# Product-key experts in one interleaved pass, and in two stages with half of the v rows read densely

## What is computed

```python
q = (hblk @ w_q).reshape(b_, PEER_BLOCK, PEER_HEADS, 2, PEER_QDIM // 2)
s1 = einsum('bthd,hnd->bthn', q[..., 0, :], k1)
s2 = einsum('bthd,hnd->bthn', q[..., 1, :], k2)
v1, i1 = lax.top_k(s1, PEER_TOPK)
v2, i2 = lax.top_k(s2, PEER_TOPK)
cand = v1[..., :, None] + v2[..., None, :]
cidx = i1[..., :, None] * PEER_NKEYS + i2[..., None, :]
score, pos = lax.top_k(cand, PEER_TOPK)      # over the 256 sums
idx = take_along_axis(cidx, pos)
gate = jax.nn.softmax(score, axis=-1)
act = jax.nn.gelu(einsum('bthkd,btd->bthk', w_u[idx], hblk))
out = einsum('bthk,bthkd->btd', gate * act, w_v[idx])
```

## Time and profile before

| | |
|---|---|
| median of 3 runs | 2938.45 us (2937.06 to 2939.99) |
| span of the profiled execution | 2939.0 us |
| first dot, last u gather | 1631.9 us, 2869.7 us |
| read from memory in the span | 898 MB |
| busy: PE, DVE, ACT, POOL | 2628.4, 1949.4, 979.2, 556.7 us |

### The profile page before, as it was taken

The page is one execution under the profiler, slowest core; times in us unless marked ns, Lnnn a source line. Parts: engine busy times, 40 slices in busy tenths (PEclk is TensorE's granted clock), DMA queues, the critical chain, the costliest instruction groups (busy, mean ns, idle before and its releaser), DMA issues.

```text
span 2939.0 us, 30782 instructions
## 1 busy us (share of the span) xinstructions
PE 2628.4 (89%) x11045; PEld 1777.7 (60%) x11045; DVE 1949.4 (66%) x2654; ACT 979.2 (33%) x1335; POOL 556.7 (19%) x580
## 2 busy tenths in 40 slices
PE   7999998999999999999999897777878877777777
PEld 3588886888777899998888753332434333232232
DVE  4679997444676788887555866666556656556646
ACT  5577776433564443334444211111101111111110
POOL 0000000000000000000000453433333333333333
PEclk9999999999999999999999999999999999999999
DMA  8733334542425888887566899999999999999998
GB/s 351 278 108 114 114 129 158 189 170 101 154 90 233 332 322 335 322 336 279 203 247 266 357 422 421 421 421 421 421 421 421 421 421 421 421 421 422 422 421 342
DMA packets 126356, 901.77 MB, mean 307 GB/s; under 512 B 14000, under 2 KB 15536, under 8 KB 17200
## 3 DMA queue, kind: packets, MB, share of 16 engines
q0 software_dynamic: 82944, 604.02, 49.8%
q1 hardware_dynamic: 38448, 276.84, 25.1%
q10 hardware_dynamic: 4864, 19.61, 1.7%
HBM read 898.29 MB, written 2.13 MB: 306 GB/s over the span
## 4 chain that ended last, share of the span: by engine, by line
PE 53%; DMA 35%; DVE 6%; issue 4%; ACT 1%; POOL 0%; POOLq 0%; SPq 0%; ACTq 0%; DVEq 0%
DMA u<-in_peer_u,idx 32%; PE ps L476 12%; PE ps L519 8%; PE ps L521 8%; PE ps L520 8%; PE ps L491 6%; DVE u L2042 3%; PE ps L882 2%; DMA v<-in_peer_v,idx 2%; PE ps L599 2%; PE ps L905 1%; DMA w<-in_stream 1%; PE ps L533 1%; PE ps L711 1%; PE ps L694 1%
## 5 line engine op out<-in xcount | busy, mean ns | idle before, releaser
L905 PE MATMUL ps<-v,dg 128*128 128x512 f32 x1920 | 894.4, 614 | 252.3 <-DMA v<-in_peer_v,idx 212.2
L2042 DVE SCALAR_TENSOR_TENSOR u<-u,hN 128x2048 f32<-128x2048 f32 x256 | 586.6, 2292 | 459.8 <-DMA u<-in_peer_u,idx 459.4
L905 PEld LDWEIGHTS ps<-v,dg 128*128 128x128 f32 x1920 | 356.4, 194 | 784.9 <-issue 427.9
L1383 DVE TENSOR_TENSOR wl<-w,wh 128x1024 fp32r<-128x1024 f32 x428 | 519.7, 1222 | 359.2 <-ACT wh L1018 358.8
L1018 ACT ACTIVATE wh<-w 128x1024 fp32r<-128x1024 f32 x428 | 451.3, 1059 | 607.9 <-PE ps L521 405.6
L2148 POOL DMA_INDIRECT u<-in_peer_u,idx x256 | 257.6, 1006 | 933.0 <-DVE u L2042 543.5
L476 PE MATMUL ps<-both,wh 128*128 128x256 f32 x2048 | 371.8, 284 | 0.0
L1326 ACT ACTIVATE dg<-con,wt 128x128 f32<-128x128 f32 x240 | 92.7, 399 | 807.4 <-PE ps L905 802.4
L476 PEld LDWEIGHTS ps<-both,wh 128*128 128x128 f32 x2048 | 320.1, 192 | 3.5 <-issue 3.3
L476 PE MATMUL ps<-both,wl 128*128 128x256 f32 x1024 | 289.8, 283 | 0.0
L2132 POOL DMA_DIRECT2D mr<-in_wmod x64 | 34.1, 534 | 1322.8 <-DVE br_lo L1791 912.7
(11 more groups left out here) (297 smaller groups left out, 2893.5 us busy)
## 6 DMA issues: line engine op xcount, KB each, us to landing
w<-in_stream SPq DMA_DIRECT2D x258, 1024.0 KB, 4.9
mr<-in_wmod POOLq DMA_DIRECT2D x64, 1024.0 KB, 6.9
wg<-in_gates ACTq DMA_DIRECT2D x8, 512.0 KB, 3.2
wx<-in_stream SPq DMA_DIRECT2D x4, 1024.0 KB, 7.9
u<-in_peer_u,idx POOLq DMA_INDIRECT x256
v<-in_peer_v,idx POOLq DMA_INDIRECT x256, 18.0
xs<-in_ctx ACTq DMA_DIRECT2D x1, 2048.0 KB, 7.6
xs<-in_x ACTq DMA_DIRECT2D x1, 2048.0 KB, 14.6
```

Source lines behind the costliest of these rows:

```text
L905: last = mm(ps[:, b, :], dg[:, k % 4, :], V[n % NV][:, b * 512:(b + 1) * 512], start=(k == 0), stop=(k == TOPK - 1))
L1383: tt(wl[p % SPLITS][:, :, :], W[s][:, q * PIECE:(q + 1) * PIECE, :], wh[p % SPLITS][:, :, :].bitcast(F32), ALU.subtract)\
L2042: stt(U[n % NU][:, :], U[n % NU][:, :], 1.0, hN[t][:, :], ALU.mult, ALU.mult, accum_out=dot[:, t, k:k + 1])\
```

## The change

The expert part is cut into two stages. In the first, only u rows are gathered, in the order of `ORDER`: both halves of head 0, then heads 1 to 7 of half 0, then those of half 1. There are eight u buffers. Of each group from the third on, the ranks 3, 8 and 13 (`ON_POOL`, without the last) are not dots of VectorE: GpSimd multiplies the tile with `hN[t]` in place (`product`), and ScalarE sums over the columns (`row_sum`). The others stay on VectorE with `U` and `hN`, both in SBUF. Results are kept in `dot` [128, 2, 128] for all heads, and weights are made once for each half.

The v table is split by columns. Its first DC = 1024 columns are read densely: 128 blocks of 128 rows x 1024 columns, in an order made on the host. For this the weights of all chosen experts are turned into a matrix for each token: index and weight tables are transposed by TensorE, VectorE makes two one-hot tiles of 128x128 for each token (`onehot`), TensorE multiplies them, and ScalarE copies four tokens at a time into `WT`. Half 0 does this between the dots of groups 9 to 15, half 1 after the last dot. Then TensorE runs 128 x 4 products of `WT` with the blocks (`dense`). The other GC = 1024 columns are gathered as before, 256 gathers of 128 rows of 4 KB into four buffers, and VectorE adds each with its weight to `acc` (`gathered`). SyncE issues the dense loads and, new, the keys and the query weights of heads 4 to 7.

```diff
+ORDER = [(0, 0), (1, 0)] + [(0, h) for h in range(1, PH)] + [(1, h) for h in range(1, PH)]
+ON_POOL = tuple(r for r in range(2 * TOPK, ROWS) if r % TOPK in (3, 8, 13) and r != ROWS - 3)
+ROUTE_AT = (1, 2, 4, 6, 7, 9, 11, 12, 14)
+TURN0 = 9
+TOKEN_AT = {n: TURN0 * TOPK + 5 + n * 103 // P for n in range(P)}
...
-        NU, NV = 4, 8
+        NU, NG, ND = 8, 4, 6
...
+            for j in range(NKEYS):
+                if j == 0:
+                    sp.wait_ge(*AR.at(PH - 1, "q"))
+                elif j == 2:
+                    sp.wait_ge(*PR.at(2 * PH - 1, "s"))
+                elif j == 4:
+                    sp.wait_ge(*VG_.at(1, "g1"))
+                elif j >= ND:
+                    sp.wait_ge(dense_done, j - ND + 1)
+                sp.dma_start(VD[j % ND][:, :], a_vd[j]).then_inc(vd_in[j % ND], 16)
...
+            def token(t, n):
+
+                m = t * P + n
+                pe.wait_ge(onehots, m + 1)
+                if m % 4 == 0 and m >= 8:
+                    pe.wait_ge(w_stored, m // 4 - 1)
+                mm(ps[:, (4, 7)[m // 4 % 2], n % 4 * P:(n % 4 + 1) * P], oa[m % 6][:, :], ob[m % 6][:, :], start=(n % 4 == 0), stop=True,
+                   skip_group_check=True).then_inc(w_made, 1)
+
+            def dense(j):
+
+                pe.wait_ge(vd_in[j % ND], 16 * (j // ND + 1))
                 for t in (0, 1):
+                    for b in range(DB):
+                        last = mm(ps[:, DB * t + b, :], WT[t][:, j, :], VD[j % ND][:, b * 512:(b + 1) * 512], start=(j == 0), stop=(j == NKEYS - 1))
...
+            def row_sum(r):
+
+                t, h = ORDER[r // TOPK]
+                c = h * TOPK + r % TOPK
+                act.wait_ge(pool_products, pool_by(r))
+                fn(U[r % NU][:, :], U[r % NU][:, :], ACT.Copy, accum_out=dot[:, t, c:c + 1]).then_inc(act_dots, 1)
...
+            def store_weights(g):
+
+                t, n = divmod(4 * g, P)
+                act.wait_ge(w_made, 4 * g + 4)
+                fn(WT[t][:, :, n:n + 4].rearrange("p i t -> p t i"), ps[:, (4, 7)[g % 2], :].rearrange("p (t i) -> p t i", t=4), ACT.Copy).then_inc(w_stored, 1)
...
+            def onehot(t, n):
+
+                m = t * P + n
+                if m >= 6:
+                    dve.wait_ge(w_made, m - 5)
+                tsc(oa[m % 6][:, :], iota_k[:, :], i1T[:, n:n + 1], None, ALU.is_equal)
+                tsc(ob[m % 6][:, :], iota_k[:, :], i2T[:, n:n + 1], wT[:, n:n + 1], ALU.is_equal, ALU.mult).then_inc(onehots, 1)
+
+            def gathered(m):
+
+                t, c = m % 2, m // 2
+                dve.wait_ge(vg_in[m % NG], 16 * (m // NG + 1))
+                if m < 2:
+                    tsc(acc[:, t, :], VG[m % NG][:, :], dot[:, t, c:c + 1], None, ALU.mult).then_inc(summed, 1)
                 else:
+                    dve.wait_ge(summed, m - 1)
+                    stt(acc[:, t, :], VG[m % NG][:, :], dot[:, t, c:c + 1], acc[:, t, :], ALU.mult, ALU.add).then_inc(summed, 1)
...
+            for r in range(ROWS):
+                q, k = divmod(r, TOPK)
+                t, h = ORDER[q]
+                if r not in ON_POOL:
+                    dve.wait_ge(u_in[r % NU], 16 * (r // NU + 1))
+                    stt(U[r % NU][:, :], U[r % NU][:, :], 1.0, hN[t][:, :], ALU.mult, ALU.mult, accum_out=dot[:, t, h * TOPK + k:h * TOPK + k + 1])\
+                        .then_inc(dve_dots, 1)
+                if (q == 0 and k) or (q == 1 and k < 14) or (q > 1 and k in ROUTE_AT):
+                    next(routes, None)
...
+            def product(r):
+
+                t, _ = ORDER[r // TOPK]
+                pool.wait_ge(u_in[r % NU], 16 * (r // NU + 1))
+                nc.gpsimd.tensor_tensor(U[r % NU][:, :], U[r % NU][:, :], hN[t][:, :], ALU.mult).then_inc(pool_products, 1)
...
+                if r >= NU:
+                    pool.wait_ge(*row_used(r - NU))
                 apart(pool)
+                nc.gpsimd.indirect_dma_start(out=U[r % NU][:, :], out_offset=None, in_=a_u,
+                                             in_offset=bass.IndirectOffsetOnAxis(ap=idx[:, q, k:k + 1], axis=0)).then_inc(u_in[r % NU], 16)
+                if r - NU + 1 in ON_POOL:
+                    product(r - NU + 1)
+
+            for m in range(ROWS):
+                t, c = m % 2, m // 2
+                if m == 0:
+                    pool.wait_ge(*VR.at(2 * PH - 1, "idx"))
+                elif m == 1:
+                    pool.wait_ge(dve_dots, dots_by(ROWS - 1))
+                elif m == 3:
+                    pool.wait_ge(*VG_.at(1, "w"))
+                elif m >= NG:
+                    pool.wait_ge(summed, m - NG + 1)
                 apart(pool)
+                nc.gpsimd.indirect_dma_start(out=VG[m % NG][:, :], out_offset=None, in_=a_vg,
+                                             in_offset=bass.IndirectOffsetOnAxis(ap=idx[:, HALF[t, c // TOPK], c % TOPK:c % TOPK + 1], axis=0)).then_inc(vg_in[m % NG], 16)
```

More of the change, by code:

```diff
@@ L47 @@
 RING = 4
+DC = 1024
+GC = D - DC
+DB = DC // 512
 PIECE = HK // 2
@@ L911, in last_half @@
[L911 to L920 removed]
+                pe.wait_ge(*VR.at(q - 2, "ib1"))
@@ new lines, in scores, with tables @@
+                pe.wait_ge(keys_in, q * 16)
+                for s in (0, 1):
+                    last = mm(ps[:, 5 + q % 2, s * NKEYS:(s + 1) * NKEYS], qT1[:, h, s, :] if t else qT0[:, (h + 1) % 6, s, :], keys[:, s, :],
+                              start=(s == 0), stop=True, skip_group_check=True)
+                last.then_inc(*PR.inc("s"))
+            def tables(t):
+                if t:
+                    pe.wait_ge(w_stored, P // 4)
+                pe.wait_ge(*VG_.at(t, "w"))
+                for i, x in enumerate((te[:, 0, t, :], te[:, 1, t, :], dot[:, t, :])):
+                    last = nc.tensor.transpose(ps[:, 4, i * P:(i + 1) * P], x, ident)
+                last.then_inc(turned_t, 1)
@@ new lines, in _ @@
+            queries(6)
+            scores(5)
+            queries(7)
+            for q in range(6, TURN0 + 4):
+                scores(q)
+            pe.wait_ge(*AR.at(PH - 1, "q"))
+            tables(0)
+            for q in range(TURN0, 2 * PH):
+                for n in range(P):
+                    if TOKEN_AT[n] // TOPK == q:
+                        token(0, n)
+                if q + 4 < 2 * PH:
+                    scores(q + 4)
+            tables(1)
+            for n in range(P):
+                token(1, n)
@@ L953, in _ @@
+            pe.wait_ge(w_stored, 2 * P // 4)
+            for j in range(NKEYS):
+                dense(j)
         @block.scalar
@@ new lines, in _ @@
+            assert next(routes, None) is None
+            gelu_inner_of(1)
+            weights_of(1)
+            copy_tables(1)
+            for n in range(P):
+                onehot(1, n)
+                if n % 8 == 7:
+                    gathered(n // 8)
+            for m in range(P // 8, ROWS):
+                gathered(m)
+            dve.wait_ge(m5_in, 16)
+            dve.wait_ge(summed, ROWS)
+            for t in (0, 1):
+                tt(acc[:, t, :], acc[:, t, :], m5r[:, DC:D], ALU.mult).then_inc(*VX.inc(f"m{t}"))
+                dve.wait_ge(*VX.at(0, f"m{t}"))
+                tt(x2[:, t, DC:D], x2[:, t, DC:D], acc[:, t, :], ALU.add).then_inc(*VX.inc(f"o{t}"))
```

581 lines of the change are left out of this document (241 added, 340 removed).

## The result

The changed kernel takes 3181.84 us in the median (3178.54 to 3184.72), the kernel before 2938.48: a ratio of 1.083, interval 1.0815 to 1.0845. The prediction was 3080, with a range of 2940 to 3190. The direction is right and the time lies near the upper end; of a loss of 243 us the forecast had 142.

A forecast was written before the change was run, and what follows sets the result against it. Transfers bound the old kernel; VectorE and GpSimd locking each other out would decide the change. First stage ends at 2498 us, seam and token work at 2582, blocks and gathers add 489, end 12: 3083, rounded to 3080; range 2940 to 3190.

The forecast's parts named there:

- The mechanism: First stage: GpSimd's products and VectorE's two-SBUF-operand dots exclude each other; 160 us of saved bytes come back as lost overlap.
- A group: First stage, 16 u rows: 49.7 us on VectorE, 51 on GpSimd, taken as 52, between 40.6 and 60.
- the hold-ups of gathers: GpSimd's line in a first-stage group: 16 gathers each delayed 0.44 us by dots, 7 us together.
- The cover of 3 us: First-stage group: about 3 us of the three products' 13.8 us pass beside routing steps and cost VectorE nothing.
- Groups with token work: Groups 9 to 13: one-hot tiles for 20 tokens add 9 us on VectorE, 58 us a group, 290 together.
- Dense products: Second stage, TensorE: 4 x 0.43 = 1.72 us a block, less than the 2.5 us of a block and gather's transfers.
- the cycle of a buffer: Gathers after the dense blocks, four buffers: 6.1 us a cycle with 3.2 landing; 1.6 us a gather, 182 for 114.
- The first: First stage: a product doesn't stop a dot, GpSimd's group takes 47 us, the whole kernel 2994 us; chance 0.19.
- the second: GpSimd keeps the transfers' pace, 41 us a group, full wire in the second stage, 2868 us in all; chance 0.14.
- The third: GpSimd falls further behind: 60 us a group, 1.9 us a gather at the end, 3229 us; chance 0.15, shared with The fourth.
- The fourth: Half rows save no time per gather: 1.9 us a piece, 358 pieces, 3274 us; chance 0.15, shared with The third.
- The mark of 41.7 us a group: First stage: below this group time, with the second stage as forecast, the changed kernel would be faster than before.

## Why the prediction was right in sign and short in size

Against the forecast's sum of 3083 the span is 100 us longer:

| step | forecast | measured | miss |
|---|---|---|---|
| first dot | 1632 | 1630.2 | -2 |
| groups 0 and 1 | 106 | 106.3 | 0 |
| groups 2 to 8 | 364 | 381.0 | +17 |
| groups 9 to 13 | 290 | 313.1 | +23 |
| groups 14 and 15 | 106 | 101.8 | -4 |
| seam and token work | 84 | 80.6 | -3 |
| blocks and gathers | 489 | 556.7 | +68 |
| end | 12 | 13.2 | +1 |

**The mechanism** was the right one: the lock is mutual, a product takes 4.50 us at least (4.6 estimated; the 4497 ns of the Trainium skill's GPSIMD Engine Reference, Performance versus the Vector engine, are met), ScalarE's sum 1.91 and 0.19, transfers are busy 78% in the first stage (80% forecast), and the 160 us of bytes come back as lost overlap.

**A group** is 55.8 us, not 52 (groups 3 to 8; group 2 takes 46.0). The run without products has 44.9 with 16 dots, so 13 dots and the steps are 44.9 - 3 x 2.21 = 38.3 (38.9 forecast). Held dots add 53 x 0.57 / 4 = 7.6, held casts 4.2: 11.8 where the sum had 13.8 - 3 = 10.8. Waits for rows add 5.6, where 52 - 49.7 = 2.3 was allowed. Together 55.7. The step that failed is "Two lines that alternate on a lock and on eight buffers don't fit perfectly; I take 52": the remainder was more than twice as large. The runs say what it is made of: products alone leave waits of 8.8 us in six groups, held gathers alone 0.2 in seven, and only both together 5.6 in each group. GpSimd's own sum was short in the same place: it put the hold-ups of gathers at 16 x 0.44 = 7 us a group, and they are 16 x (1.756 - 0.940) = 13. The cover of 3 us was nearly right (products of 14.75 us a group by 59.0 / 4, less 11.8), though not as thought: the searches run beside a product, but the routing's own cast is held by it.

**Groups with token work** were put at 58 us, by VectorE's line alone (38.9 + 10.8 + 9 = 58.7). Groups 10 to 13 take 61.5 each, group 9, in which the weights of half 0 are made, 67.2. Their own addition is right, 9.1 us without products (54.0 - 44.9, forecast 9). What failed is the cover of 3 us: in groups 10 to 13 dots, tiles, table instructions and casts last 14.0 us a group longer than the same ones without products, more than the 13.5 us that three products last by themselves, and VectorE waits for no row. 38.3 + 9.1 + 14.0 are 61.4.

**Dense products** were mis-sized by a factor of two. "64 products in 27.48 us" counted records; the changed kernel has 1024 records for 128 x 4 = 512 products, so a product of 128x512 in f32 leaves two, and 441 us / 512 are 0.86 us at a granted clock of 1.00 (2.4 GHz), 3.45 us a block and not 1.72. By chance the forecast's figure for the lower clock (3.44 us) is the same number; the clock wasn't lower. This didn't move the changed kernel's end (the run with half of them), but it set a floor for every repair of it.

**The second stage** is where most of the miss lies, and the failed term is the cycle of a buffer, which the run with more buffers shows: with eight of them from the 113th gather on, the same blocks and gathers take 497 us instead of 557. It took a landing of 3.2 us from a 512 KB direct load. The gathers' own row behind the dense blocks (issues from 3060 to 3160, median us to landing):

```profile
vg<-in_v_rows,idx POOLq DMA_INDIRECT x51, 5.4
```

The last 58 sums take 115.5 us, 1.99 each. So a cycle of four takes 8.0 us, not 6.1, and a gather 1.99 instead of 1.6. In the forecast's own order the run with half of the products shows it undisturbed: 324 us for the blocks (307 forecast), then 225 for the rest (182), 60 of the 68 us. With full dense products it is 441 + 116, and so the forecast's sign "dense products ended about 180 us before the last weighted sum" was not met.

**The rivals.** The first (no mutual exclusion, 2994) and the second (2868) are refuted by the traces: all 11 dots that began while a product ran ended 2.15 to 2.16 us behind it, and a group takes 55.8 us, not 41. The third got its 1.9 us a gather at the end nearly right, but not its 60 us a group. The fourth asked for 1.9 us a piece: 122 blocks and 181 gathers pass in 441 us, 1.46 a piece, and 1.28 at 409 GB/s with buffers enough, so halves do save their bytes. The mark of 41.7 us a group, below which the kernel would be faster, was reached by single groups but by no run's mean: 43.3 us with the operand in PSUM and three products, 44.9 with VectorE alone.

## What to carry to other kernels

Before work is moved from VectorE to GpSimd, list all of VectorE's instructions that would run beside it, the small ones too: each with two SBUF operands, and each cast or tensor-scalar, can wait for a whole product; put one operand into PSUM, or don't move the work. Splitting a mixed pass into stages takes away the overlap that paid for it; sum each stage by its own slowest engine, and size a ring by the landing of its own kind of transfer. When a duration is read from a count, settle first how many records one instruction leaves.

## What the hardware showed that was not expected

- Held instructions are small ones too: a cast of 128x32 takes 4394 ns in the mean instead of 162, a two-operand instruction of 128x16 takes 3864 instead of 174, tensor-scalars of 128x128 take 620 and 581 instead of 286 and 351, one of 128x16 takes 3117 instead of 170. Searches were never held: in the changed kernel seven MAX8 of 128 columns and the FIND_INDEX8 behind them ran while a product did, at their usual lengths (293 to 298 and 289 to 291 ns).
- Of a dot and a product that begin close together, the recorded start doesn't tell which one waits: a lead of up to 0.53 us didn't save the dot, one of 0.77 or more did.
- A gather issued beside two-operand dots takes 2078 ns, beside dots with one operand in PSUM 936; the total time was the same (3057.19 and 3059.14 us), for VectorE was the bound.
- A busy share of 0.98 was not a full wire: 366 GB/s with four buffers, 409 with eight or ten. It was 408 with four as well, from 2700 to 2930 us of the run with half of the dense products, where the blocks' own loads came faster. Rows of 4 KB beside dense blocks peaked at 409, rows of 8 KB before at 421.
